# A mixture of experts on slots of one expert (23 steps, indexed rows) in place of slots of one group (28 steps)

## The reference, cut to what matters

```python
def hierarchical_moe(h, w_rg, b_rg, w_re, b_re, w_gate, w_up, w_down):
    g_prob = jax.nn.softmax(ht @ w_rg + b_rg)
    g_val, g_idx = lax.top_k(g_prob, 1)                     # 1 of 4 groups
    e_in = take(e_logits.reshape(-1, 4, 4), g_idx)          # its 4 experts
    e_val, e_idx = lax.top_k(jax.nn.softmax(e_in), 2)       # 2 of 4
    gate = g_val * e_val / jnp.sum(e_val)
    combine = sum(one_hot(4 * g_idx + e_idx, 16) * gate)    # (512, 16)
    a = jnp.einsum('td,edf->tef', ht, w_gate)               # 16 x (1024, 256)
    u = jnp.einsum('td,edf->tef', ht, w_up)
    hid = jax.nn.silu(a) * u * combine[..., None]
    return jnp.einsum('tef,efd->td', hid, w_down)           # 16 x (256, 1024)
```

## Time and profile before

| | us |
|---|---|
| median of 3 runs (lowest, highest) | 1744.39 (1741.7, 1758.29) |
| profiled execution | 1744.98 |
| its span, first to last instruction | 1743.2 |
| TensorE busy | 1655.1 (95%), 7715 matmuls |
| VectorE, ScalarE busy | 875.6 (50%), 775.9 (45%) |
| GpSimd busy | 125.0 (7%) |
| DMA | 247.82 MB, 142 GB/s in the mean |

### The profile page before, as it was taken

One profiled execution on the slowest core, in us unless ns is written; L12 is line 12 of the kernel. 1 busy time (PEld: TensorE's weight loads), 2 busy tenths in 40 slices (PEclk: granted clock), 3 DMA queues, 4 the chain that ended last, 5 costly groups with the idle time before them and its releaser, 6 DMA issues.

```text
span 1743.2 us, 20038 instructions
## 1 busy us (share of the span) xinstructions
PE 1655.1 (95%) x7715; PEld 1308.7 (75%) x7715; DVE 875.6 (50%) x1010; ACT 775.9 (45%) x901; POOL 125.0 (7%) x87
## 2 busy tenths in 40 slices
PE   6999999999998889859999999999999999999998
PEld 5777777887876777647688888876788688888886
DVE  6434434444577777747642342421355665565464
ACT  5553454223467666727443343351223543443333
POOL 2101101000222223210010000000000000000000
PEclk8999999999999999979999999999999999999999
DMA  7456553223599999931421211131323133333322
GB/s 226 133 188 222 193 179 123 77 82 125 168 342 346 355 330 323 327 139 49 143 68 49 73 57 64 62 110 49 121 87 105 51 97 105 89 96 98 95 79 67
DMA packets 183202, 247.82 MB, mean 142 GB/s; under 512 B 10236, under 2 KB 151000, under 8 KB 179808
## 3 DMA queue, kind: packets, MB, share of 16 engines
q1 hardware_dynamic: 178911, 232.21, 40.4%
q0 software_dynamic: 4224, 14.72, 2.1%
HBM read 233.23 MB, written 13.67 MB: 142 GB/s over the span
## 4 chain that ended last, share of the span: by engine, by line
PE 78%; DVE 9%; DMA 5%; ACT 4%; issue 2%; SPq 1%; POOL 0%; ACTq 0%; DVEq 0%; POOLq 0%
PE psum L409 20%; PE psum L410 19%; PE psum L411 19%; DMA raw_more<-in_w_up 4%; DVE w_lo_more L1699 3%; PE psum L2466 2%; ACT w_hi_more L1694 1%; PE psum L709 1%; DVE w_lo L1699 1%; DVE pre L488 1%; PE psum L792 1%; PE psum L1203 1%; PE psum L1437 1%; PE psum L1204 1%; PE psum L1205 1%
## 5 line engine op out<-in xcount | busy, mean ns | idle before, releaser
L409 PE MATMUL psum<-h_hi,w_hi 128*128 128x512 f32 x1160 | 466.0, 402 | 7.7 <-DVE w_lo L386 3.2
L411 PE MATMUL psum<-h_hi,w_lo 128*128 128x512 f32 x1160 | 453.5, 391 | 0.0
L410 PE MATMUL psum<-h_lo,w_hi 128*128 128x512 f32 x1160 | 453.4, 391 | 0.0
L386 DVE TENSOR_TENSOR w_lo<-raw,w_hi 128x2048 fp32r<-128x2048 f32 (+2 forms) x99 | 223.7, 2259 | 228.4 <-ACT w_hi L382 228.4
L409 PEld LDWEIGHTS psum<-h_hi,w_hi 128*128 128x128 f32 x1160 | 218.4, 188 | 69.4 <-issue 18.4
L411 PEld LDWEIGHTS psum<-h_hi,w_lo 128*128 128x128 f32 x1160 | 218.6, 188 | 46.9
L410 PEld LDWEIGHTS psum<-h_lo,w_hi 128*128 128x128 f32 x1160 | 218.8, 189 | 46.4 <-issue 3.6
L382 ACT ACTIVATE w_hi<-raw 128x2048 fp32r<-128x2048 f32 (+2 forms) x100 | 187.9, 1879 | 75.3 <-PE psum L411 70.0
L1699 DVE TENSOR_TENSOR w_lo_more<-raw_more,w_hi_more 128x2048 fp32r<-128x2048 f32 x41 | 115.0, 2804 | 50.0 <-ACT w_hi_more L1694 50.0
L439 ACT ACTIVATE sq<-x 128x512 f32<-128x512 f32 x56 | 35.4, 632 | 161.0 <-DVE x L1316 105.2
L1694 ACT ACTIVATE w_hi<-raw 128x2048 fp32r<-128x2048 f32 x42 | 80.4, 1914 | 35.7 <-DMA raw<-in_w_up 16.6
(11 more groups left out here) (380 smaller groups left out, 2595.4 us busy)
## 6 DMA issues: line engine op xcount, KB each, us to landing
raw<-in_w_up SPq DMA_DIRECT2D x72, 512.0 KB, 6.5
wm_raw<-in_w_mod SPq DMA_DIRECT2D x24, 1024.0 KB, 5.9
raw<-in_w_in SPq DMA_DIRECT2D x18, 1024.0 KB
raw<-in_w_in SPq DMA_DIRECT2D x33, 512.0 KB
raw<-in_w_gate SPq DMA_DIRECT2D x28, 512.0 KB, 5.1
raw_more<-in_w_down SPq DMA_DIRECT2D x28, 512.0 KB, 6.2
raw<-in_w_down SPq DMA_DIRECT2D x28, 512.0 KB, 5.9
raw_more<-in_w_gate SPq DMA_DIRECT2D x27, 512.0 KB, 5.0
```

What stands on the lines that cost most here:

```text
L386: dve.tensor_tensor(w_lo[j][:, 0:tiles, :], raw[j][:, 0:tiles, :], w_hi[j][:, 0:tiles, :].bitcast(F32), ALU.subtract).then_inc(G["lo_ready ...
L409: pe.matmul(to, w_hi[j][:, tile, :], hi_k, start=(k == 0), stop=False)
L410: pe.matmul(to, w_hi[j][:, tile, :], lo_k, start=False, stop=False)
L411: return pe.matmul(to, w_lo[j][:, tile, :], hi_k, start=False, stop=last)
```

## The change

It works on pairs of a token and one of its two experts: 1024 pairs, sorted by expert. A slot of 128 rows now belongs to one expert. 16 slots are fixed, one for each expert; 7 take what exceeds 128 pairs of an expert (fewer than 8 can be needed). Each slot is one step, so `STEPS = SLOTS = 23`, and 69 units of weights are loaded and split instead of 84. The expert of steps 16 to 22 is read from `table`.

Rows are taken and put by index. SP stores `h_tok` once in token order (`h_rows`). GpSimd gathers a slot's rows from it (`gather`), and scatters its outputs to `y_rows`, one row for each pair (`store_y`); an index that lies outside the array (an unfilled row of a slot) moves nothing. Both are now done in every step. The index lists come from a new chain of VectorE operations and small products: `hot` (place in the slot), `in_slot`, and `coded` (token and pair number), multiplied on TensorE. The products with a permutation for slot 0 are gone; slot 0 is gathered like the others. Zero fills at the start are gone.

In each step TensorE turns the next slot's tokens, ScalarE makes `s_hi`, VectorE `s_lo`. Since a slot's sum is complete after one step, VectorE copies it out in every step (`copy_y` moves from ScalarE to VectorE), and the next down product waits for that copy. GpSimd splits the down unit of every step except the last two (21 units). The last slot is not scattered: its rows are split and multiplied by `last_pick` (one column of 512 for each token), and added to x; then the two rows of each token are loaded (4.2 MB), added together, turned and added.

The core of the diff:

```diff
-SLOTS = T // P + GROUPS - 1
-STEPS = SLOTS * PER_GROUP
+EXTRA = PAIRS // P - 1
+SLOTS = EXPERTS + EXTRA
+STEPS = SLOTS
...
-            dve.memset(zeros, 0.0).then_inc(W["wm_silu"], 1)
...
-            for i in range(SLOTS):
-                pool.dma_start(sorted_h[i * P:(i + 1) * P, :], zeros).then_inc(W["zero_out"], 16)
...
+            for m in range(TOP * NT):
+                dve.tensor_scalar(hot[:, m, :], const_row(RC_PLACE, P), places[:, m:m + 1], None, ALU.is_equal)\
+                   .then_inc(E["e_hot"], 1)
+            dve.wait_ge(E["e_matched"], LISTED)
+            listed = psum[:, ROUTE_BANK, LIST0:LIST0 + 2 * SLOTS]
+            dve.tensor_copy(at_row[:, :, :], listed.rearrange("p (v s) -> p v s", v=2)).then_inc(E["e_routed"], 1)
...
-        POOL_UNITS = [unit_down(n) for n in range(1, STEPS - 1, 2)]
+        POOL_UNITS = [unit_down(n) for n in range(STEPS - 2)]
...
+            def store_tokens():
+                to = h_rows.rearrange("(i p) d -> p i d", p=P)
+                for half in range(2):
+                    sp.wait_ge(G["h_hi_ready"], 8 * N_MOE + 4 * half + 4)
+                    sp.dma_start(to[:, :, half * T:(half + 1) * T], h_tok[:, :, half * T:(half + 1) * T])\
+                      .then_inc(E["e_stored"], 16)
...
+            def gather(s):
+                if s >= 2:
+                    pool.wait_ge(E["e_turned"], tokens_turned(s - 2))
+                pool.indirect_dma_start(hg[s % 2][:, :], None, h_rows,
+                                        bass.IndirectOffsetOnAxis(ap=at_row[:, 0, s:s + 1], axis=0),
+                                        bounds_check=T - 1, oob_is_err=False).then_inc(E[f"e_hg{s % 2}"], 16)
+
+            def store_y(s):
+                pool.indirect_dma_start(y_rows, bass.IndirectOffsetOnAxis(ap=at_row[:, 1, s:s + 1], axis=0),
+                                        y_sb[:, :], None, bounds_check=PAIRS - 1, oob_is_err=False)\
+                    .then_inc(E["e_ystore"], 16)
...
             for n in range(STEPS):
-                s, e = n // PER_GROUP, n % PER_GROUP
+                if n + 2 < SLOTS:
+                    gather(n + 2)
+                if n:
+                    pool.wait_ge(E["e_ycopy"], n)
+                    store_y(n - 1)
                 if unit_down(n) in POOL_UNITS:
                     unit_lo(pool, unit_down(n))
...
             def down(n):
-                if e == 0:
-                    if s:
-                        pe.wait_ge(E["e_ycopy"], s)
+                if n:
+                    pe.wait_ge(E["e_ycopy"], n)
...
             for n in range(STEPS):
                 gate_up(n, 0)
                 if n:
                     turn_hidden(n - 1)
-                if n % PER_GROUP == 2 and n // PER_GROUP + 1 < SLOTS:
-                    turn_tokens(n // PER_GROUP + 1)
+                if n + 1 < SLOTS:
+                    turn_tokens(n + 1)
                 gate_up(n, 1)
                 if n:
                     down(n - 1)
...
+            def copy_y(n):
+                dve.wait_ge(E["e_used"], unit_down(n) + 1)
+                dve.wait_ge(E["e_ystore"], 16 * n + 16)
+                dve.tensor_copy(y_sb[:, :].rearrange("p (b t) -> p b t", b=2), psum[:, Y_BANK:Y_BANK + 2, :])\
+                   .then_inc(E["e_ycopy"], 1)
...
                 dve_lo(3 * n + 4)
+                if n:
+                    copy_y(n - 1)
                 dve_lo(3 * n + 5)
                 dve.wait_ge(E["e_hi"], hidden_turned(n))
...
-                if e == 1 and s + 1 < SLOTS:
-                    tokens_lo(s + 1)
+                if n + 2 < SLOTS:
+                    tokens_lo(n + 2)
                 dve_lo(3 * n + 6)
...
+            for half in range(2):
+                cols = slice(half * T, (half + 1) * T)
+                dve.wait_ge(E[f"e_hg{half}"], 16 * ((SLOTS + 1 - half) // 2 + TOP))
+                dve.tensor_tensor(y_back[:, 0, :, cols], y_back[:, 0, :, cols], y_back[:, 1, :, cols], ALU.add)\
+                   .then_inc(E["e_chain"], 1)
```

484 lines of the change are left out of this document (271 added, 213 removed).

## The result

| | before | after |
|---|---|---|
| median (lowest, highest), us | 1749.45 (1741.7, 1758.29) | 1787.52 (1783.45, 1789.04) |
| span of the profiled execution | 1743.2 | 1785.8 |
| the stage: first matmul of the first gate product to last matmul of the last down product (starts) | 471.86 to 757.33: 285.5 | 473.33 to 798.47: 325.1 |

The changed kernel is slower: ratio 1.0227, 95% interval 1.0191 to 1.0264. That is 38 us by the medians and 42.6 by the spans; forecast were 23.6. The side is right, the size is not. (The forecast started from 1744.4, the median of three runs.)

What follows compares the result with a forecast made beforehand. It took VectorE's and GpSimd's mutually exclusive weight splits, in a loop with copy_y, scatter and down product, to set the step: 1745 + 21 (stage) + 2 (routing) + 0 (way back) = 1768 us, range 1722 to 1803.

Steps and rivals of the forecast that it cites:

- the splits exclude each other: Expert stage: VectorE and GpSimd do not split weights at the same time; the second waits for the first.
- the ring: Expert stage: loop of copy_y, scatter, GpSimd's split and down product; 10.4 us without any wait of GpSimd for VectorE.
- The head: Routing before the expert stage: at_row at 461, first product at 469.5 to 473; 2 us added, ends -1 and +5.
- The way back: From the last expert product back into x: adds start some 17 us after the end; 0 change, ends -3 and +4.
- the step, 13.6 us forecast: Expert stage: 13.0 us a step plus 0.6 for the slow clock, ends 12.4 and 15.3; stage 306 us, +21.
- GpSimd first: Step where GpSimd's split ends before VectorE's: copy_y ends at Q+7.4, GpSimd's next split at Q+13.5, or Q+14.2 to Q+15.4.
- Q: Expert stage: the moment GpSimd ends its split, from which the prediction counts the times within a step.
- VectorE first: Step where g_lo is past when GpSimd's split ends: copy_y ends 4.3 us later, GpSimd's next split 10.5 us later.
- The bytes set the pace: Rival: the expert stage goes by bytes (79 MB, 246 us) or product, exclusion not mattering; 1708 us, chance 0.18.
- Slow clock throughout: Rival: GpSimd first each time and TensorE's clock down in each step, 15.3 us; +57, 1804 us, chance 0.16.
- VectorE usually first and the clock holding: Rival: same loop in the expert stage at 12.4 us a step; 1743 us, no change, chance 0.22.
- The scatter's landing: Rival: copy_y waits for the previous scatter, deciding only from 11.5 us landing; at 15 us, 1829 us; no chance of its own.

Runs made afterwards that it cites:

- plain: The changed kernel with each gather by index replaced by a plain load of 128 consecutive (wrong) rows: 1788.42 us, ratio to before 1.0233.
- early: The changed kernel with each gather issued a turn sooner, ahead of the scatter: 1793.15 us, ratio to before 1.0267.
- none_early: The changed kernel with no split on GpSimd (VectorE splits all 69 units) and each gather issued a turn sooner: 1716.14 us, ratio to before 0.9826.
- order_early: The changed kernel with GpSimd's 21 splits each put ahead of the scatter and each gather issued a turn sooner: 1726.48 us, ratio to before 0.9873.

## Why the prediction came out short

**Right.** That the splits exclude each other, that the ring copy_y, scatter, split, down product sets the step, that GpSimd's split follows a scatter in each step, and that the DMA share falls to about 0.7 (0.69). The head: at_row 461 (460.92 for the gather's issue), 2.0 for the issue (2.21), first product by 473 (473.33), so 1.5 us more where 2 were taken. The way back: from the last down product to the next norm's first product 27.0 us before (757.33 to 784.29) and 25.9 after (798.47 to 824.39); 0 was taken. The bytes of the stage: 79 MB forecast, 78.57 moved.

**Wrong: the step, 13.6 us forecast.** The mechanism was right, its size was not. From the first scatter of the stage (500.59) to the last but one (789.27) there are 20 steps, 288.7 us; without the one of 19.3 they are 14.2 in the mean. For two steps in which VectorE's split meets GpSimd's, the prediction had 14.2 to 15.4 and 10.5, which is 12.4 to 13.0 a step; it took 13.0, and 0.6 for the clock. The pair above took 16.2 and 12.4, 14.3 a step. The terms that were too small:

- The end of copy_y in the "GpSimd first" step: Q+8.65 where the sum had Q+7.4. Of this 0.5 is VectorE's own queue, and 0.75 the wait for a down product that came late: TensorE had waited for hg, and lost another 1.6 us to the low clock behind that wait. The sum had no term for hg inside the stage. So VectorE's next split began at Q+9.4, where Q+8.9 was the latest that the sum had, and GpSimd's behind it took 5.74.
- The low clock in the "VectorE first" step: 1.6 us, which is 0.8 a step over the pair. 0.6 a step was taken, for slow down products; the other down product of the pair ran at the high clock, and the low one stood ahead of it, as just said.
- The hand-over on GpSimd: 0.81 from copy_y to the scatter and 0.02 from the scatter to the split, where the sum had 0.3 and 0.3; 0.2 a step. The 0.3 came from one DMA issued right behind another, not from one that waits for another engine.

The pair is 0.8 and 1.9 us above its two terms, 2.7 in all or 1.3 a step, against the 0.6 that was added: 0.7 short, and 0.6 in the mean of the stage. In other pairs the parts differ (at 649.74 hg was late by 5.1 us, and the down product behind it ran at the high clock).

**Missing: SP's wait for last_pick.** The changed kernel has it in SP's queue (L1688), ahead of all later loads, where the kernel before waited for an early turn of tokens; the sum has no term for it. 19.3 - 13.6 = 5.7 us.

So the stage: 19 steps x 0.58 = 11.0, the stall 5.7, and the first and last steps 2.4, give the 19.1 us between 306 and 325.1.

**Missing: the gather.** Its landing of 9.4 us, against the 6.5 taken for the first one, did make TensorE wait for hg, as the last sentence of the prediction feared. plain and early show that there is nothing to gain from it alone while the ring stands: a gap ahead of the down product and the low clock took its place.

**The rivals.** "The bytes set the pace" was given 0.18; it is what the same change gives once GpSimd splits nothing: 249 us in none_early where 246 were worked out. It needed the ring and the exclusion gone, not only one of them. "Slow clock throughout, 15.3 us a step" is too high by 1.1; the granted clock of the stage was 0.87. "VectorE usually first and the clock holding, 12.4 us a step" is too low by 1.8: its two kinds of step are there, but longer (16.2 and 12.4 in the pair), and the clock did not hold. The scatter's landing, 4.9 us here, was far from the 11.5 at which it would decide; it came to matter only in the runs without the ring.

## What to carry to other kernels

When an engine takes over a piece of work, ask what its queue waits for just ahead of that piece: here a split that had waited for nothing but its weights came to wait for a scatter, which waits for the product that the split itself feeds. Before moving work, put the free piece ahead of the waiting one in the queue; that was worth 47 us of 325. And the longest wait in a list is not the price of its cause: cut it and read where the wait goes. Copy_y was left on VectorE in all runs; what the ring costs with it back on ScalarE was not tried. The version to keep of those run here is none_early (1716.14 us, 0.9826 of before), and order_early (0.9873) if GpSimd is to split.
